# Third mixer of a four-layer f32 network: forget gates first, two weight splits ahead of the spread factor, row tiles in the recurrences

## What is computed

```python
qa, ka, va, qb, fb, ib, gb = jnp.split(y @ w_in, EVEN_SPLITS, axis=-1)
oa = chunk_band_attention(rope(qa), rope(ka), va, ...)
f = lbh + (1.0 - lbh) * sigmoid(fb)          # forget gate
cum = cumsum(log(f), within blocks of 32)     # 16 blocks of 32 tokens
q_dec, k_end = qb * exp(cum), (1 - f) * exp(last - cum)
o_intra = masked product inside each block
def step(state, xs):                          # one per block of 32
    o = q_dec @ state
    state = exp(last) * state + k_end.T @ ib  # einsum('blhd,blhe->bhde', ke, vv)
ob = rmsnorm(o_intra + o) * norm_w * silu(gb)
out = concat(oa, ob) @ w_out
```

## Time and profile before

| | before |
|---|---|
| median of 3 runs | 2418.6 us (2417.28 to 2418.71) |
| profiled execution, its own time | 2418.93 us |
| its span in the trace | 2417.1 us |
| PE busy / DVE / ACT / POOL | 91% / 45% / 35% / 30% |
| mean granted PE clock | 0.947 of 2.4 GHz |
| even mixer, first projection to last recurrence | 941.6 to 1235.1 us of the span |

### The profile page before, as it was taken

The page is one execution under the profiler, slowest core; times in us unless marked ns, Lnnn a source line. Parts: engine busy times, 40 slices in busy tenths (PEclk is TensorE's granted clock), DMA queues, the critical chain, the costliest instruction groups (busy, mean ns, idle before and its releaser), DMA issues.

```text
span 2417.1 us, 29698 instructions
## 1 busy us (share of the span) xinstructions
PE 2210.8 (91%) x11372; PEld 1695.8 (70%) x11372; DVE 1078.0 (45%) x1783; ACT 843.5 (35%) x1561; POOL 727.4 (30%) x446
## 2 busy tenths in 40 slices
PE   6899988899999998898888999998997788999996
PEld 5888555588555545786666888886885566888885
DVE  1520888513355522455534625253116724625252
ACT  2322656323344423245113323224116633322232
POOL 1221000242000002230542444444443342444442
PEclk8899999999999999798889999999998989999998
DMA  6221333132000012220022333332331121333331
GB/s 244 68 63 44 93 92 93 49 105 62 18 1 1 1 37 71 68 80 18 1 61 61 105 96 93 100 90 59 105 93 31 36 62 53 105 96 94 100 90 57
DMA packets 255745, 168.62 MB, mean 70 GB/s; under 512 B 5760, under 2 KB 247143, under 8 KB 254455
## 3 DMA queue, kind: packets, MB, share of 16 engines
q1 hardware_dynamic: 251792, 157.31, 22.1%
q0 software_dynamic: 2192, 8.45, 1.1%
q10 hardware_dynamic: 1623, 0.98, 0.1%
HBM read 164.57 MB, written 2.14 MB: 69 GB/s over the span
## 4 chain that ended last, share of the span: by engine, by line
PE 75%; issue 11%; DVE 7%; POOL 3%; ACT 2%; ACTq 0%; DMA 0%; DVEq 0%; POOLq 0%
PE ps L348 17%; PE ps L349 16%; PE ps L350 16%; PE ps L504 7%; PE ps L612 5%; PE ps L576 3%; POOL WL L1227 2%; PE ps L1331 2%; PE ps L976 1%; DVE MX L517 1%; PE ps L555 1%; PE ps L401 1%; PE ps L983 1%; DVE PT L594 1%; PE ps L477 1%
## 5 line engine op out<-in xcount | busy, mean ns | idle before, releaser
L1227 POOL TENSOR_TENSOR WL<-raww,WH 128x1024 fp32r<-128x1024 f32 (+1 forms) x239 | 564.0, 2365 | 903.9 <-ACT WH L303 859.1
L348 PE MATMUL ps<-HH,WH 128*128 128x512 f32 (+1 forms) x1368 | 529.1, 387 | 46.7 <-DVE HL L447 19.5
L349 PE MATMUL ps<-HL,WH 128*128 128x512 f32 (+1 forms) x1368 | 524.2, 383 | 0.0
L350 PE MATMUL ps<-HH,WL 128*128 128x512 f32 (+1 forms) x1368 | 523.1, 382 | 0.0
L303 ACT ACTIVATE WH<-raww 128x1024 fp32r<-128x1024 f32 (+1 forms) x239 | 244.7, 1034 | 320.1 <-PE ps L350 320.0
L348 PEld LDWEIGHTS ps<-HH,WH 128*128 128x128 f32 x1368 | 263.2, 192 | 107.1 <-issue 28.7
L350 PEld LDWEIGHTS ps<-HH,WL 128*128 128x128 f32 x1368 | 262.6, 192 | 50.0
L349 PEld LDWEIGHTS ps<-HL,WH 128*128 128x128 f32 x1368 | 263.4, 193 | 47.7
L529 ACT ACTIVATE PB<-ps,NB 128x256 f32<-128x256 f32 (+5 forms) x256 | 167.7, 655 | 102.3 <-DVE NB L518 64.3
L576 PE MATMUL ps<-ident,PB 128*128 128x128 f32 x952 | 157.7, 283 | 23.3 <-DVE PT L594 16.1
L514 DVE TENSOR_REDUCE NB<-ps 128x1 f32<-128x768 f32 (+4 forms) x128 | 92.5, 722 | 128.6 <-PE ps L504 127.6
(11 more groups left out here) (281 smaller groups left out, 3366.6 us busy)
## 6 DMA issues: line engine op xcount, KB each, us to landing
raww<-in_ffn_w_up SPq DMA_DIRECT2D x88, 512.0 KB, 3.9
raww<-in_ada_w SPq DMA_DIRECT2D x32, 512.0 KB, 3.5
raww<-in_ffn_w_down SPq DMA_DIRECT2D x32, 448.0 KB, 3.7
raww<-in_odd_w_in SPq DMA_DIRECT2D x24, 512.0 KB, 3.8
raww<-in_even_w_in SPq DMA_DIRECT2D x21, 512.0 KB, 3.8
raww<-in_a_w_in SPq DMA_DIRECT2D x20, 512.0 KB, 3.7
raww<-in_ffn_w_down SPq DMA_DIRECT2D x16, 512.0 KB, 3.9
ADA<-in_ada_w SPq DMA_DIRECT2D x6, 1024.0 KB, 10.0
```

The costliest lines, as they stand in the source:

```text
L348: nc.tensor.matmul(out, lh, rh, start=start and k == ks[0], stop=False)
L349: nc.tensor.matmul(out, lh, rl, start=False, stop=False)
L350: ins = nc.tensor.matmul(out, ll, rh, start=False, stop=stop and k == ks[-1])
L1227: nc.gpsimd.tensor_tensor(lo, raw_slot(k), hi.bitcast(F32), ALU.subtract).then_inc(*split_lo.mark(k))
```

## The change

Three edits. (1) The forget gates' panels come first in the even mixer, in the panel list and on PE, ACT and DVE; keys, queries and values follow. (2) `late_root_act` splits two further panels, the sixth between root and copy of the spread factor, the seventh right after the copy, in all four places. (3) The recurrences' L1505 becomes 16 matmuls for each head (L1509), each on 32 partitions at its own row position of the array (`tile_position`) and into its own bank; POOL's masked copies are gone, and all sixteen signal once, on the last.

```diff
+        cols("e_f", we, 1280, 4)
         cols("e_k", we, 512, 1)
         cols("e_q", we, 0, 4)
...
-        cols("e_f", we, 1280, 4)
...
-        def late_root_act(act, st):
+        def late_root_act(act, st, first):
             act.wait_ge(*statted[st, 8])
             nc.scalar.activation(STAT[:, 0, 0:4], ps[:, 7, 0:4], ACT.Sqrt, bias=oned[:, 3:4])\
                 .then_inc(*rms_made.mark(st))
+            ahead(act, first, 5)
             act.wait_ge(*rinv_made[st, 0])
             nc.scalar.activation(R2B, bank(("rinv", st, 0)), ACT.Copy).then_inc(*act_out.mark("r2", st))
+            ahead(act, first, 6)
...
         def even_pe(pe):
-            lin_pair(pe, [("ek", ("e_k", 0), 0, lambda m, s: (dve_out, ("raw", "ek", 0))),
-                          ("eq", ("e_q", 0), 0, lambda m, s: (dve_out, ("raw", "eq", 0)))], h_at, LAT,
+            lin_pair(pe, [("ef", ("e_f", m), m, lambda m, s: (dve_out, ("efr", m))) for m in range(2)], h_at, LAT,
                      lambda k: h_made["s00", k], "s00")
-            for m in range(1, 4):
+            for m in range(2, 4):
+                lin(pe, "ef", ("e_f", m), m, h_at, LAT, lambda m, s: (dve_out, ("efr", m)))
+                if m == 2:
+                    late_stat(pe, "s00")
+            late_spread(pe, "s00")
+            lin(pe, "ek", ("e_k", 0), 0, h_at, LAT, lambda m, s: (dve_out, ("raw", "ek", 0)))
+            for m in range(4):
                 lin(pe, "eq", ("e_q", m), m, h_at, LAT, lambda m, s: (dve_out, ("raw", "eq", m)))
...
-                for t in range(NT):
-                    b = lin_bank(("gd", n, t))
-                    claim(pe, b, (dve_out, ("st", n, t)))
-                    pe.wait_ge(*pool_out["vb", n, t])
-                    nc.tensor.matmul(ps[:, b, :], g_ke[:, t, :], g_vb[:, t % 2, :], start=True, stop=True)\
-                        .then_inc(*grouped.mark("gd", n, t))
+                for q in range(4):
+                    claim(pe, lin_bank(("gd", n, q)), (dve_out, ("st", n, 3)))
+                for t in range(NT):
+                    for q in range(4):
+                        rows = slice(32 * q, 32 * q + 32)
+                        ins = nc.tensor.matmul(ps[:, values[("bank", ("gd", n, q))], t * P:(t + 1) * P], g_ke[rows, t, :],
+                                               e_i[rows, t, n * P:(n + 1) * P], start=True, stop=True,
+                                               tile_position=(32 * q, 0))
+                ins.then_inc(*grouped.mark("gd", n))
...
+            for m in range(4):
+                act.wait_ge(*dve_out["efr", m])
+                nc.scalar.activation(e_f[:, m, :], e_f[:, m, :], ACT.Sigmoid).then_inc(*act_out.mark("ef", m))
+                ahead(act, ("e_f", m), 3)
+            ahead(act, ("e_k", 0), 3)
+            for m in range(4):
                 ahead(act, ("e_q", m), 3)
...
-            hgrn_values(pool)
```

More of the change, by code:

```diff
@@ L1500, in hgrn_pe @@
                 pe.wait_ge(*act_out["ket", n])
-                for t in range(NT):
-                    b = lin_bank(("gd", n, t))
-                    claim(pe, b, (dve_out, ("st", n, t)))
-                    pe.wait_ge(*pool_out["vb", n, t])
-                    nc.tensor.matmul(ps[:, b, :], g_ke[:, t, :], g_vb[:, t % 2, :], start=True, stop=True)\
-                        .then_inc(*grouped.mark("gd", n, t))
+                if n == 0:
+                    for i in range(2):
+                        pe.wait_ge(*act_out[f"ei{i}", 3])
+                for q in range(4):
+                    claim(pe, lin_bank(("gd", n, q)), (dve_out, ("st", n, 3)))
+                for t in range(NT):
+                    for q in range(4):
[5 more added lines that the diff above has]
+                for t in range(NT):
                     if n and t == 1:
@@ L1701, in scalar_program @@
             norm_sqrt(act, "nf", 8, 4)
-            ahead(act, ("e_k", 0), 2)
+            ahead(act, ("e_f", 0), 2)
             late_parts_act(act, "s00", lambda k: x_made["nf", k], 0)
-            ahead(act, ("e_k", 0), 4)
-            late_root_act(act, "s00")
+            ahead(act, ("e_f", 0), 4)
+            late_root_act(act, "s00", ("e_f", 0))
             act.wait_ge(*dve_out["lbd"])
             nc.scalar.activation(LB[:, 1:3, :], LB[:, 1:3, :], ACT.Exp).then_inc(*act_out.mark("lbe"))
-            for m in range(2, 4):
+            for m in range(4):
[4 more added lines that the diff above has]
+            for m in range(4):
                 ahead(act, ("e_q", m), 3)
@@ L1713, in scalar_program @@
             ahead(act, ("e_v", 0, 1), 3)
[L1714 to L1717, removed]
             hgrn_act_gates(act)
@@ L1739, in scalar_program @@
             ahead(act, ("o_k", 0), 4)
-            late_root_act(act, "s10")
+            late_root_act(act, "s10", ("o_k", 0))
             for m in range(8):
@@ L2048, in even_dve @@
             dve.wait_ge(rope_in[2], 16)
+            for m in range(4):
+                late_scaled(dve, e_f[:, m, :], ("ef", m, "lat"), ("efr", m), "s00")
             late_scaled(dve, raw[0], ("ek", 0, "lat"), ("raw", "ek", 0), "s00")
@@ L2056, in even_dve @@
                          made=dve_out)
-            for m in range(4):
-                late_scaled(dve, e_f[:, m, :], ("ef", m, "lat"), ("efr", m), "s00")
             dve.wait_ge(*act_out["lbe"])
@@ L2128, in hgrn_dve @@
             hgrn_gated(dve, 3)
-        def hgrn_values(pool):
-            for n in range(4):
-                for t in range(NT):
[L2134 to L2138, removed]
-                                                      rotm[:, 0, b:b + 1], None, ALU.mult)
-                    ins.then_inc(*pool_out.mark("vb", n, t))
         def hgrn_gated(dve, n):
@@ L2151, in states @@
         def states(dve, n, t):
-            dve.wait_ge(*grouped["gd", n, t])
+            dve.wait_ge(*grouped["gd", n])
             for b4 in range(4):
```

12 lines of the change are left out of this document (3 added, 9 removed).

## The result

The changed kernel takes 2385.5 us (median of 4 runs, 2384.2 to 2386.7), the one before 2418.65 in the same session: a ratio of 0.9864, 95% interval 0.9852 to 0.9876, so 33 us faster. The forecast was 2379, with a range from 2367 to 2396. The profiled execution took 2386.74 us with a span of 2384.9, 32.2 less than the span of before.

The account below looks back on a forecast made before the run. PE, busy 91% of the span, was taken to bound the kernel through its waits and low clock. Projections 21, row tiles 12 and splits 7 made 40 us: 2418.9 - 40 = 2379, range 2367 to 2396.

Parts of the forecast that it names:

- Projections: Forget gates first: PE's wait ahead of the values, their low clock, panels behind and fourth "eqb" wait together win 21.0 us.
- the fourth "eqb" panel: Projections: PE's wait of 3.67 us for its low part becomes 2.8, winning 0.9 us; bounds 5.4 won, 1 lost.
- The rival of values at the low clock: Projections: the values' clock stays low, about 10 + 1 us are not won, 2390 in all; chance 0.15.
- Row tiles: Recurrences: row tiles without POOL's masked copies win 12 us, bounds 5 and 18.
- First head: Recurrences: no wait for POOL, and wide products faster or no longer between the state steps, 6 us in all.
- last head: Recurrences: POOL's splits run early, so DVE's L2148 of 6.75 us goes back to about 0.7, winning 6.1.
- I take 0 for each of the three: Recurrences, heads two to four: no gain or loss in each, bounds +2 and -2.5 us.
- The rival had the clock right: Recurrences: row tiles run singly at 0.50, sixteen taking 6.8 us; some 9 us less won, 2388; chance 0.10.
- the 0.06 to 0.11 that I had named as the sign: Recurrences: L1509 should show 0.06 to 0.11 us per record; over 0.2 would mean the prediction is wrong.
- The 3.5 us that I set against the change: Recurrences: by the skill's load rule a head's sixteen tiles take 3.5 us, no less than the four wide products before.
- Splits in the FFNs: Both FFNs: no wait at the sixth panel, waits of 2 to 2.5 us return; 7 us won, bounds 3 and 11.8.
- The 2.9 us of low clock: Second FFN: low clock behind the sixth panel's wait, 7.19 - 19 x 0.226 = 2.9 us, counted as saved.

Follow-up runs that it names:

- e1: Kernel before the change with only the gates' panels first and, in this mixer only, the two early splits: 2398.7 us, ratio 0.9917.
- e2: Kernel before the change with only the row tiles and no masked copies: 2407.6 us, ratio 0.9956.
- e4: Changed kernel, with POOL's three splits ahead of the output projection held until DVE has written the third head's normed output: 2391.2 us, ratio 0.9884.
- e12: Changed kernel, with only ACT's split of the fourth "eqb" panel moved ahead of the gates' last Exps: 2371.7 us (2 runs), ratio 0.9800.
- e6: Changed kernel with 8 extra products of 512 columns ahead of the last projections of the third and fourth mixer: 2391.3 us, one run.
- e7: Changed kernel with 16 extra products of 512 columns ahead of the last projections of the third and fourth mixer: 2396.6 us, one run.
- e8: Changed kernel with ACT's splits moved at three places: fourth "eqb" panel, both FFNs, end of the first FFN: 2366.1 us, ratio 0.9786.
- e3: Kernel before the change with only the two early splits, in both FFNs and the fourth mixer: 2411.9 us, ratio 0.9977.
- e10: Changed kernel with eight added products of 32 columns behind the row tiles in each head: 2386.1 us, ratio 0.9854.

## Why the prediction came out right, and where it was off

**Projections: 21.0 forecast, 21.4 measured.** Each term is found: 9.1 for the wait, 9.8 for the values (9.9), about 1 for the first panels behind them, 1.4 for the fourth "eqb" panel (0.9). The rival of values at the low clock did not occur: entered without a wait, they run at 1.00. e1 confirms the term alone.

**Row tiles: 12 forecast, 9.1 measured** (10.3 in e2), the term that was furthest off. First head 5.8 (6) and last head 6.5 (6.1) are right, and e4 shows the mechanism for 4.0 of the last. The step that failed is "I take 0 for each of the three": heads two and three lost 1.5 and 1.8 us, inside the bound of 2.5. With the same row tiles they lost 0.2 together in e2 and gained 1.8 together in e12, so the size of this step hangs on the clock that the heads get, which the sum held fixed. The rival had the clock right (0.50) and the tiles wrong. Side by side they take 1.17 us at the full clock, 0.037 per record, less than the 2 us that I took and under the 0.06 to 0.11 that I had named as the sign; it is everything around them, L1529 above all, that pays for the clock. The 3.5 us that I set against the change (less than the 3.9 of the four wide products, not "no less") came from taking the sixteen loads one after the other. The rule of the Trainium skill that a load costs by its columns ("TensorE: Matmul & The Clock Gate", LDWEIGHTS) does not say that they are, and the trace shows that they overlap; the measured factor of 3.07 on the same page of the Trainium skill (Measured speedup vs the span model) gave an estimate of 1.3, near the 1.17.

**Splits in the FFNs: 7 forecast, 6.4 measured.** The waits come back at the eighth and ninth panel as 0.34 + 1.53, against 2 to 2.5 forecast. The first FFN gives 3.3, as worked out; the second 3.1, not 4 or more. The 2.9 us of low clock that I counted there are right. The stretch of 19 records in the earlier trace rows ends before the panel does; the whole panel, with its 24 records, takes 8.43 in the kernel before, 3.0 over 24 x 0.226 = 5.4:

```profile
2053.81:2062.24 8.43, 8.43 (x24) 6.67 (x25) 6.89 (x8) 3.15 (x4) 3.56 (x2) 0.64 0.22 64
```

Up to its last norm the second FFN does gain 4.2 (2392.30 - 2015.92 = 376.4 us from its first record before, 2359.02 - 1986.87 = 372.2 after). What it loses again, 1.1, stands at its end, where no edit is: the eight records that spread the last norm's factor ran at the full clock before and run at the low one now, and the 32 transposes behind them take 5.97 in place of 5.80. Before, then after:

```profile
2392.30 1.16 PE L477 MATMUL ps<-ident,STAT 128*128 128x128 f32 x8 [0.70 <-DVE STAT L468]
```

```profile
2359.02 2.07 PE L479 MATMUL ps<-ident,STAT 128*128 128x128 f32 x8 [0.70 <-DVE STAT L470]
```

**What was not in the sum: 6.1 us lost in stages without an edit.** I took the clock of a stage to be its own. e6, e7, e8 and e12 show that it depends on what stands ahead of the stage: the third attention is between 51.3 and 56.5 us long in kernels that have the same code for it. With this the 40 us of the forecast came out as 32.2 in the trace and 33 by the medians. That the time lies inside the range all the same is in part luck: the range was set by the rivals, and none of them was this one. What decides the clock of a stage at a given moment isn't settled: the start of the third mixer scatters by 4 us between executions without changing the attention or the recurrences of e8 against e12 or of before against e3, yet e10, the same code as the changed kernel up to the recurrences, has an attention of 52.8 and not 53.6.

## What to carry to other kernels

Order independent projections so that those whose readers are slow (a rope, a chain of scans) don't stand right ahead of a step that claims many banks; put those with a cheap reader first. When replacing wide products by small ones on an engine whose clock can fall, count the clock of everything in that stretch, not only the new instructions. And count a few us either way for stages behind an edit: compare stage by stage before giving an edit the credit or the blame. Where a stretch shows fewer records than the code has, look at the records behind it before calling them missing: the stretch may end too early.

## What the runs showed of the hardware that was not expected

- Sixteen 32-row tiles with 128 columns (32 records) take 1.17 us at a granted clock of 1.00 and 2.09 at 0.50: they do run side by side.
- 96 matmuls of 128 columns stay at 1.00 when entered there (10.44 us) and stay at 0.50 when entered at 0.50 (20.50 us): in this stage the thin work kept the level that it found. In the recurrences it did not always (0.72 and 0.61 in the second head of e2 and of the changed kernel). Heads two and three with wide products of 512 columns among their work were at 0.81 to 0.94 in six traces, those without at 0.50 to 0.74 in eight.
- POOL's split of two SBUF tiles stretches a DVE cast of one SBUF tile from 0.43 to 2.45 us and a subtraction of two from 0.69 to 2.71, while state steps with one SBUF tile and PSUM keep their 0.38.
- The clock of a stage hangs on the work ahead of it: the same code for the third attention takes 51.3 us at 0.87 and 56.5 at 0.71.
